# A Hyena block's FFT as matrix products: the inverse transform in unsplit float32 instead of three passes of split halves

## The reference, cut to what matters

```python
def hyena_mixer(u, w_in, b_in, conv_w, conv_b, ...):
    z = short_conv(u @ w_in + b_in, conv_w, conv_b)
    x0, x1, v = jnp.split(z, 3, axis=-1)
    s = (v * x1).astype(jnp.float32)
    g = hyena_filter(L, ...)
    n = 2 * L
    y = jnp.fft.irfft(jnp.fft.rfft(s, n=n, axis=1) * jnp.fft.rfft(g, n=n, axis=0)[None], n=n, axis=1)[:, :L]
    y = (y + s * skip) * x0
    return y @ w_out + b_out
...
x = x + mixed          # x is first_block(...), whose last step is rms_norm(h, g_final)
```

## Time and profile before

| What | us |
|---|---|
| median of 3 runs (1584.76 to 1591.93) | 1588.11 |
| the profiled execution: its time | 1584.69 |
| its span in the trace | 1582.8 |
| TensorE busy (94%) | 1494.4 |
| VectorE busy (59%) | 937.3 |
| ScalarE busy (35%) | 560.6 |
| GpSimd busy (10%) | 154.0 |

### The profile page before, as it was taken

One profiled execution on the slowest core, in us unless ns is written; L12 is line 12 of the kernel. 1 busy time (PEld: TensorE's weight loads), 2 busy tenths in 40 slices (PEclk: granted clock), 3 DMA queues, 4 the chain that ended last, 5 costly groups with the idle time before them and its releaser, 6 DMA issues.

```text
span 1582.8 us, 17881 instructions
## 1 busy us (share of the span) xinstructions
PE 1494.4 (94%) x6672; PEld 1190.3 (75%) x6672; DVE 937.3 (59%) x1218; ACT 560.6 (35%) x740; POOL 154.0 (10%) x161
## 2 busy tenths in 40 slices
PE   6999998889998999999999999988899999999995
PEld 5677666667886888888888778865778888888884
DVE  6776666664543577547636787677775443443445
ACT  4321562442333354323314454442243322221232
POOL 1000131220000000000000022264500000000000
PEclk8899999889998999999999999998899999999997
DMA  5222115124220223222222332222122323322221
GB/s 206 89 75 84 69 54 186 41 80 184 83 80 27 80 80 106 86 101 102 84 107 80 106 105 101 87 93 93 39 95 80 106 80 107 106 80 106 81 106 53
DMA packets 24524, 146.79 MB, mean 93 GB/s; under 512 B 2820, under 2 KB 5017, under 8 KB 9102
## 3 DMA queue, kind: packets, MB, share of 16 engines
q1 hardware_dynamic: 19726, 127.94, 22.9%
q0 software_dynamic: 4016, 15.68, 2.9%
q10 hardware_dynamic: 720, 2.30, 0.4%
HBM read 139.61 MB, written 6.30 MB: 92 GB/s over the span
## 4 chain that ended last, share of the span: by engine, by line
PE 83%; DVE 7%; ACT 3%; issue 2%; DMA 1%; SPq 1%; POOL 1%; DVEq 0%; ACTq 0%; POOLq 0%
PE ps L1464 25%; PE ps L1465 25%; PE ps L1466 25%; DMA raw<-weights_dram 1%; DVE w_lo L820 1%; SPq L305 1%; PE ps L1803 1%; ACT w_hi L465 1%; PE ps L1790 1%; PE ps L1644 1%; PE ps L1565 1%; DVE opA_lo L863 1%; DVE gen L1123 1%; PE ps L1653 1%; PE ps L1695 1%
## 5 line engine op out<-in xcount | busy, mean ns | idle before, releaser
L1464 PE MATMUL ps<-opA_hi,w_hi 128*128 128x512 f32 x1184 | 472.9, 399 | 15.4 <-DVE opA_lo L871 11.8
L1465 PE MATMUL ps<-opA_lo,w_hi 128*128 128x512 f32 x1184 | 469.8, 397 | 0.0
L1466 PE MATMUL ps<-opA_hi,w_lo 128*128 128x512 f32 x1184 | 467.5, 395 | 0.0
L465 ACT CAST w_hi<-raw 128x2048 fp32r<-128x2048 f32 x111 | 211.2, 1903 | 374.3 <-PE ps L1466 369.9
L820 DVE TENSOR_TENSOR w_lo<-raw,w_hi 128x2048 fp32r<-128x2048 f32 x112 | 258.7, 2310 | 134.8 <-ACT w_hi L465 124.5
L1464 PEld LDWEIGHTS ps<-opA_hi,w_hi 128*128 128x128 f32 x1184 | 224.5, 190 | 74.6 <-DVE w_lo L820 12.6
L1466 PEld LDWEIGHTS ps<-opA_hi,w_lo 128*128 128x128 f32 x1184 | 224.1, 189 | 51.8
L1465 PEld LDWEIGHTS ps<-opA_lo,w_hi 128*128 128x128 f32 x1184 | 223.7, 189 | 51.9 <-issue 1.4
L1464 PE MATMUL ps<-opB_hi,w_hi 128*128 128x512 f32 x576 | 230.6, 400 | 18.2 <-issue 6.2
L1465 PE MATMUL ps<-opB_lo,w_hi 128*128 128x512 f32 x576 | 229.8, 399 | 0.0
L1466 PE MATMUL ps<-opB_hi,w_lo 128*128 128x512 f32 x576 | 228.5, 397 | 0.0
(11 more groups left out here) (325 smaller groups left out, 1625.9 us busy)
## 6 DMA issues: line engine op xcount, KB each, us to landing
raw<-weights_dram SPq DMA_DIRECT2D x118, 1024.0 KB, 4.8
g_dram<-gen POOLq DMA_DIRECT2D x8, 512.0 KB, 3.4
h<-x_t_dram SPq DMA_DIRECT2D x4, 512.0 KB, 11.5
h<-x_t_dram POOLq DMA_DIRECT2D x1, 2048.0 KB, 11.1
scores<-g_dram POOLq DMA_DIRECT2D x4, 512.0 KB, 3.9
g_spec<-g_dram POOLq DMA_DIRECT2D x4, 512.0 KB, 3.6
out_dram<-h ACTq DMA_DIRECT2D x4, 512.0 KB, 2.7
mem_raw<-mem_t_dram POOLq DMA_DIRECT2D x1, 1024.0 KB, 10.7
```

Of the source, the lines that this page charges most:

```text
L465: A.copy(w_hi[:, p, :], raw[:, p, :]).then_inc(hi_ready, 1)
L1464: W.matmul(out, w[0], x[0], start=start, stop=False, skip_group_check=mixed)
L1465: W.matmul(out, w[0], x[1], start=False, stop=False, skip_group_check=mixed)
L1466: return W.matmul(out, w[1], x[0], start=False, stop=stop, skip_group_check=mixed)
```

## The change

1. **The inverse is not split.** The products of the spectrum's four parts are left in float32: GpSimd writes them to `y_spec[0]` and `y_spec[1]` (in the places of opA_hi and opA_lo), and TensorE multiplies them with a float32 table `inv` in one pass, q inside and c outside, so that each c ends on its own. ScalarE's roundings, VectorE's and GpSimd's low halves and the split of the table are gone. The even part has 257 columns and starts at column 255 of its bank (258 from column 254 before).
2. **GpSimd** makes the two sums for each n and nothing else here. The residual is scaled by VectorE in the tail of hy_out, one more instruction for each of 8 tiles; the loads of g go to SyncE's queue.
3. **Order.** TensorE: forward 0 to 7, inverse(0), inverse(1), hy_out. VectorE: all eight sets of products, then for each c value and low half, one after the other. `inv` lies in the upper 8 KB of w_lo (slot 1), so the second weight slot for hy_out is split only after `inv_done` reaches 8; the first before c = 4.
4. **Loads.** The forward table comes in four transfers over all 128 partitions; its special row comes apart, in two small transfers of GpSimd's queue to `mid_row`, and ScalarE copies it in. One weight pair for hy_out is loaded into raw slot 1 before the inverse table, the other into slot 0 after it.
5. The row of frequency 0 is patched by ScalarE in y_spec (two copies for each half) instead of by VectorE.
6. w_hi, w_lo and what lies behind them start at multiples of 128 bytes again (before: shifted by 32 and 64 bytes, since the table had 2052 columns).

```diff
-        w_hi = at("w_hi", [P, 2, 2 * CHUNK], F32R, 96 * KB + 32)
-        w_lo = at("w_lo", [P, 2, 2 * CHUNK], F32R, 112 * KB + 64)
+        w_hi = at("w_hi", [P, 2, 2 * CHUNK], F32R, 96 * KB)
+        w_lo = at("w_lo", [P, 2, 2 * CHUNK], F32R, 112 * KB)
+        inv = at("inv", [P, 2 * CHUNK], F32, 120 * KB)
+        y_spec = [at("y_spec0", [P, KT, T], F32, 16 * KB), at("y_spec1", [P, KT, T], F32, 32 * KB)]
...
@@ gpsimd @@
-            pool.wait_ge(first_rstd, 1)
-            for k in range(KT):
-                nc.gpsimd.tensor_tensor(h[:, k, :], h[:, k, :], acc_next[:], ALU.mult).then_inc(h2_scaled, 1)
...
+                t, y = spec[:, n % 2], y_spec[n // 4]
+                pool.wait_ge(fs_read, n + 1)
+                nc.gpsimd.tensor_tensor(y[:, 2 * (n % 4), :], t[:, 0, :], t[:, 1, :], ALU.subtract).then_inc(spec_sum, 1)
+                nc.gpsimd.tensor_tensor(y[:, 2 * (n % 4) + 1, :], t[:, 2, :], t[:, 3, :], ALU.add).then_inc(spec_sum, 1)
...
@@ vector @@
                 if n >= 2:
-                    dve.wait_ge(y_hi, 2 * n - 2)
-                    dve.wait_ge(y_lo, n - 1)
-                    dve.wait_ge(y_lo_im, n - 1)
+                    dve.wait_ge(spec_sum, 2 * n - 2)
+                if n in (2, 6):
+                    dve.wait_ge(row_zero, 2 + n // 6 * 2)
...
+            for n in range(8):
+                spectrum_products(n)
+            V.engine_nop().then_inc(bank_read, 4)
+            for c in range(KT):
+                if c == 4:
+                    split_after(F_PAIR)
+                hyena_value(c)
+                if c:
+                    hyena_out_lo(c - 1)
+                if c == 6:
+                    dve.wait_ge(inv_done, 8)
+                    split_after(I_PAIR)
+            hyena_out_lo(KT - 1)
...
@@ tail, for hy_out @@
+                        S.link(V.scalar_tensor_tensor(h[:, k, :], h[:, k, :], vec("g_final", k), first_scale[:], ALU.mult, ALU.mult))
...
@@ tensor, inverse(half), for each c @@
+                        if q == 0:
+                            first = W.matmul(bank[:, HALF - 1:T], y_re, inv[:, EC:EC + HALF + 1], start=True, stop=False,
...
+                            W.matmul(bank[:, HALF - 1:T], y_im[0:1], nyq_row[:], start=False, stop=False, skip_group_check=True)
...
+                            last = W.matmul(bank[:, HALF:T], y_im, inv[:, at_e:at_e + HALF], start=False, stop=q == 3,
...
-            for n in range(6):
+            for n in range(8):
                 forward_s(n)
...
             inverse(0)
-            forward_s(6)
-            forward_s(7)
             inverse(1)
```

More of the change, by code:

```diff
@@ L302, in _ @@
                 for r in range(2):
[L303 to L308, removed]
-            sp.wait_ge(lo_ready, I_PAIR - 1)
@@ L315, in _, with load_spectrum @@
-            with sp.Fori(I_PAIR // 2 + 1, PIPE // 2) as m:
+                    sp.dma_start(dst[:, :, r], src[:, :, r, 0:2, :]).then_inc(fwd_in, 16)
+            def load_spectrum(n):
+                sp.dma_start(g_spec[n % 2].rearrange("p a t -> p (a t)"), g_dram[n // 4, n % 4]).then_inc(g_back[n % 2], 16)
+            sp.wait_ge(summed, 32)
+            for p in range(2):
+                sp.wait_ge(g_out[p], 64)
+            load_spectrum(0)
+            sp.wait_ge(lo_ready, F_PAIR)
+            sp.dma_start(raw[:, 1, :], a["weights"][I_PAIR + 1 + PAIRS - PIPE + 1]).then_inc(raw_in[1], 16)
@@ L316, in _ @@
+            sp.wait_ge(lo_ready, F_PAIR + 1)
+            sp.dma_start(raw[:, 0, :], a["weights"][I_PAIR + 1 + PAIRS - PIPE]).then_inc(raw_in[0], 16)
+            for n in range(2, 8):
+                sp.wait_ge(fs_read, n - 1)
+                load_spectrum(n)
+            with sp.Fori(I_PAIR // 2 + 2, PIPE // 2) as m:
                 for p in range(2):
@@ L736, in hy_taps @@
                 if isinstance(i, int) and 2 * (m + 1) == F_PAIR:
-                    (inv_hi_part if p else fwd_hi)()
+                    if p == 0:
+                        fwd_hi()
                 else:
@@ L1304, in hy_conv @@
                     V.tensor_tensor(z_pad[:, p, j, 1:1 + T], ps[:, 2 * p + j, :], rstd[:], ALU.mult).then_inc(bank_read, 1)
[L1305 to L1308 removed]
+                if not (isinstance(i, int) and p and 2 * (m + 1) == F_PAIR):
                     split_lo(m + 1, p)
@@ new lines, in inverse @@
+                y = y_spec[half]
+                for c in range(4):
+                    cs = slice(c * P, (c + 1) * P)
+                    bank = ps[:, 4 + c, :]
+                    if half:
+                        pe.wait_ge(inv_read, c + 1)
+                    for q in range(4):
+                        if c == 0:
+                            pe.wait_ge(spec_sum, 8 * half + 2 * q + 2)
+                            if q == 0:
+                                pe.wait_ge(row_zero, 2 * half + 2)
+                        y_re, y_im = (y[:, 2 * q + f, cs] for f in range(2))
+                        if q == 0:
+                            first = W.matmul(bank[:, HALF - 1:T], y_re, inv[:, EC:EC + HALF + 1], start=True, stop=False,
+                                             skip_group_check=True)
+                            if half and c == 0:
+                                first.then_inc(chunk_done, 4)
+                            W.matmul(bank[:, HALF - 1:T], y_im[0:1], nyq_row[:], start=False, stop=False, skip_group_check=True)
+                        elif q == 1:
+                            W.matmul(bank[:, HALF - 1:T], y_re, inv[:, EC + HALF + 1:EC + 2 * (HALF + 1)], start=False, stop=False,
+                                     skip_group_check=True)
```

269 lines of the change are left out of this document (84 added, 185 removed).

## The result

The changed kernel takes **1546.42 us** (median of 4, 1545.88 to 1548.55) against 1589.55 for the kernel before in the same session (median of 4, 1584.76 to 1591.93): a ratio of 0.9735, 95% interval 0.9709 to 0.9761. The forecast was 1561 with a range of 1552 to 1574. So the sign was right and the gain too small: in the two profiled executions 38.7 us of span (1582.8 to 1544.1) instead of 27.0.

What follows compares the result with a forecast made beforehand. TensorE was taken as the bound, losing idle time and clock in the Hyena stage: 90.4 us before, 0.45 + 29.5 + 33.5 = 63.45 after, gain 27.0. That gave 1557.7, or 1561.1 on the median's footing; forecast 1561, range 1552 to 1574.

Steps and rivals of the forecast that it cites:

- the line on addresses: Weight tiles w_hi and w_lo, formerly 32 and 64 bytes off: shifting their addresses was taken to be worth 0.
- Stall taken: 0: Forward transform: no wait of TensorE for PSUM banks; bound above 2 us, and 3 more if g(2) queues behind 2 MB.
- Rival A: Forward transform: the ring of two buffers sets the pace, or inverse table and g(2) queue up; 1570 us, chance 0.12.
- Hand-over: From hy_in's last transposes to the forward transform: TensorE idle 0.45 us instead of 6.20, bounds 0 and 6.20.
- Forward: Both halves of the forward transform on TensorE at full clock: 29.5 us.
- Inverse: Unsplit inverse on TensorE: 0.217 us per record, 0.71 for the one-row pair, 4.18 per c, 33.5 us for eight.
- VectorE beside the inverse: VectorE needs 3.3 us per c against TensorE's 4.18, so hy_out starts at once.
- the scaling: Residual's scaling on VectorE in hy_out's tail: 6.0 us of work, cost 0, bound 6.0 if all on the path.
- B: Tail of hy_out: VectorE falls behind with all eight scalings on the path, + 6.0 us, 1567; chance 0.05.
- C: Inverse: records writing 257 columns from odd PSUM column 255 take twice as long, 10.4 us, 1571; chance 0.05.
- D: Inverse: weight loads not hidden under the matmul before, 27.4 us eating the gain, 1588, no change; chance 0.03.
- E: From forward(0) to hy_out: the clock stays low, + 56 us, 1617; chance 0.05, with anything else not seen.

Runs made afterwards that it cites:

- reordered loads: The change with SyncE's queue reordered, the second weight pair and the inverse table going out before g(1); 1538.65 us.
- both scaling runs: The change with the residual's scaling made twice by VectorE, 1546.85 us; the change with it made by GpSimd again, 1545.08 us.
- the kernel with only the rest moved: The change with only the small tiles and what lies behind them at their old 32-byte remainder, w_hi and w_lo unmoved; 1545.94 us.
- The run on the hand-over: The kernel before with only the forward table's loads as in the change; 1580.38 us against 1591.17, ratio 0.9914.

## Why the prediction missed, step by step

**The failed step is the line on addresses**, "w_hi now lies 32 bytes off, w_lo 64, and both give the same 0.231 in rows 6; I take 0 for the shift". The reading was right and the conclusion wrong: two shifted tiles that cost the same say nothing of an unshifted one, and no row of before showed one. The term should have had a bound on the side of a gain: each 0.001 us of distance is 5.3 us over the 5280 fast 128x512 matmuls of the program, since TensorE is the bound almost everywhere. Measured: 0.2311 to 0.2267, which is 23 us by that count, and 18.5 us of the medians. Most of what lies between them is the clock: in the trace with the old addresses the stall in the forward transform brought no slow matmuls (see the last section), which spared that kernel 3.3 us. Its stretches give 13.8 us ahead of the transforms (with the head's scatter in it), 0.4 in the forward transform and 8.4 behind, 22.6 in all.

**The second one is "Stall taken: 0".** The text had the cause ("if g(2) stands behind the inverse table and a weight pair (2 MB in the same queue), 3 more") as a bound, and the order of the queue stood in the listing. It came: 2.60 us idle. Rival A's mechanism was right in its second half, the queue, with the slow clock behind it; its first half was not, as the ring of two buffers was long enough once the queue was in order. In the sum for the transforms, 6.2 us more than the 63.45 (with the 0.4 of a hand-over):

| Term | forecast | measured |
|---|---|---|
| hand-over | 0.45 | 0.40 |
| forward, without the stall (reordered loads) | 29.5 | 1080.04 - 1050.73 = 29.31 |
| stall | 0 | 2.60 |
| slow clock behind it | 0 | 35.18 - 2.60 - 29.31 = 3.27 |
| inverse | 33.5 | 1123.10 - 1089.07 = 34.03 |

- *Hand-over:* right, cause and size.
- *Forward:* the count was right; the shorter distance (some 0.4 us less) makes up for what little I had left out.
- *Inverse:* a product takes 0.43 us (1121.56 - 1121.13), two records of 0.215, where the earlier trace rows gave 0.217. The one-row part was 0.12 too small: 1120.70 - 1119.01 = 1.69 for L1833, L1838 and L1850, less 2·0.43, is 0.83 against 0.71. By the four passes that the Trainium skill, "FP8 and Floating Point Precision", TensorE Precision Notes, gives true FP32, each taken as long as a fast pass in the stream, an estimate is 0.48, and 2.9 us more for the stage; here the row decided, and rightly. The 0.43 does not speak against four passes, though: it is 4.0 cycles of 2.4 GHz for each of the 256 columns, so only the 0.12 for one pass was too long for them.
- *VectorE beside the inverse, the scaling, the second weight slot:* TensorE is busy for 70.93 of the 70.93 us from 1089.07 to 1160, and two runs say the scaling is free. No run has the unsplit inverse alone, without the new order of the loops: what it costs TensorE and what it frees on VectorE are read from the stage as a whole.
- *Rivals:* B fell (both scaling runs); C fell, L1833 and L1840 are 378 ns long in the mean as L1844 is, and L1840 and its follower lie 0.43 apart; D fell by the same distance; E did not come.

With 18.5 us for the addresses and 5.9 for the stall put in, the forecast of 1561.1 becomes 1548.5; with 22.6 for the addresses it becomes 1544.4. Measured was 1546.42.

## What to carry to other kernels

Never price a shift of a hot operand's address at zero from rows in which all are shifted: look at the distance between matmuls in a steady window of both kernels, and multiply by their number. Count distances from start to start, not matmuls in a window. Keep what TensorE loads as weights and what it streams at a distance of a whole multiple of 512 bytes (as here, with tiles 16 KB apart), and give way to an odd table size elsewhere. When loads move to another queue, write down the issue order with bytes: a small load that is waited for belongs ahead of the large one that is not.

## What was not expected of the hardware

- **The distance between fast fp32r matmuls depends on where the weight tile lies relative to the moving operand**: 0.2267 us at 0, 0.2311 with w_lo alone or two unlike shifts of 32 to 128 bytes, 0.2333 with two equal shifts of 64 or 128 bytes. The weight loads themselves are not recorded longer: 1187.1 us in sum in the change and 1184.3 with the old addresses, while the busy time of the matmuls grows from 1473.5 to 1493.7. The Trainium skill, "SBUF — State Buffer", Who interferes with whom, has contention only at the port pair that VectorE and GpSimd share. That rule alone would give one distance for all these kernels; the measurements differ by 3%. Whether TensorE's two reads collide is not shown, only that their relative place counts.
- **A stall of nearly the same length does or does not bring the slow clock.** In the change, 2.60 us of idle time were followed by a mean clock of 0.62 over 8.98 us (first fence). With the old addresses the stall at the same place was 2.29 us and the clock stayed at 1.00:

```profile
1084.96:1094.00 9.04, 9.04 (x34) 5.90 (x35) 4.73 (x8) 0.00 (x0) 5.93 (x5) 1.00 0.37 121
```

  In the run with w_lo + 128 it was 2.57, and the forward transform took 32.2 us in all, too short for slow matmuls (35.2 with them). Two runs had a stall of 2.36 us: w_lo + 64 kept its clock, and the kernel with only the rest moved did not (35.06 us for the forward transform). With w_hi + 32 and w_lo + 64 alone, 2.52 us of idle time were followed by 10.2 us at the lower clock, and the forward transform took 36.80 us, 4.5 more than its stall and the 29.74 us of the run with all old addresses, less its stall. So a price for "idle, then slow" is idle plus 0 to 4.5 us here; which of them comes could not be told from the length of the stall. The run on the hand-over adds one: its wait of 2.02 us at the output projection left the clock at 1.00, where a wait of 2.00 us in the kernel before was followed by the 0.54 of the earlier trace rows.
